# Smaller weight transfers for experts 2 to 7 and larger ones for the last two experts, in a decoder layer with routed experts

## The reference, cut to what matters

```python
h = h + merged @ w_out[l]                       # the mixer's end
logits = xt @ w_router + b_router               # 32 experts, 4 per token
top_val, top_idx = lax.top_k(logits, TOP_K)
gates = jax.nn.softmax(top_val)
def expert_block(xb, e):
    hdn = xb @ w_up[e] + b_up[e]                # 1024 -> 2048
    x_glu = jnp.minimum(hdn[:, :D_FF], 7.0)
    x_lin = jnp.clip(hdn[:, D_FF:], -7.0, 7.0)
    act = x_glu * sigmoid(1.702 * x_glu) * (x_lin + 1.0)
    return act @ w_down[e] + b_down[e]          # 1024 -> 1024
h = h + sum over the 4 experts of gate * expert(h)
out = rms_norm(h)[:, 16:]
```

## Time and profile before

| | before |
|---|---|
| median of 3 runs | 1183.54 us |
| profiled execution | 1183.1 us, span 1181.2 us |
| granted TensorE clock, mean | 0.992 |
| PE busy | 1146.4 us (97%) |
| DVE, ACT busy | 228.2 us (19%), 188.3 us (16%) |
| queue of SP (q1) | 439.19 MB, 88.1% of 16 engines' span |
| waits of PE's products for transfers (L881, L900) | 14.0 us in all, none before 700 us |

### The profile page before, as it was taken

One profiled execution on the slowest core, in us unless ns is written; L12 is line 12 of the kernel. 1 busy time (PEld: TensorE's weight loads), 2 busy tenths in 40 slices (PEclk: granted clock), 3 DMA queues, 4 the chain that ended last, 5 costly groups with the idle time before them and its releaser, 6 DMA issues.

```text
span 1181.2 us, 13320 instructions
## 1 busy us (share of the span) xinstructions
PE 1146.4 (97%) x5598; PEld 532.9 (45%) x5598; DVE 228.2 (19%) x527; ACT 188.3 (16%) x406; POOL 0.2 (0%) x4
## 2 busy tenths in 40 slices
PE   9999999999999999999999999999999999998996
PEld 7767888855343333333343433333333333333332
DVE  4555620114111111111111111111111111111112
ACT  2257620002011110101010111101010101010102
POOL 0000000000000000000000000000000000000000
PEclk9999999999999999999999999999999999999999
DMA  9834434487999999999999999999999999999996
GB/s 378 341 148 179 150 110 166 151 336 295 396 414 436 432 427 432 432 431 432 433 432 431 433 433 428 435 433 427 434 435 427 434 434 428 434 434 427 428 426 261
DMA packets 26128, 442.03 MB, mean 374 GB/s; under 512 B 4144, under 2 KB 4656, under 8 KB 7408
## 3 DMA queue, kind: packets, MB, share of 16 engines
q1 hardware_dynamic: 23472, 439.19, 88.1%
q10 hardware_dynamic: 2624, 2.39, 0.6%
HBM read 440.52 MB, written 1.05 MB: 374 GB/s over the span
## 4 chain that ended last, share of the span: by engine, by line
PE 73%; DMA 25%; ACT 1%; DVE 0%; issue 0%; ACTq 0%; SPq 0%; another core or an unknown queue 0%; DVEq 0%
PE ps L881 28%; DMA ring<-in_w_exp_dram 17%; PE ps L900 12%; PE ps L539 11%; DMA work<-in_w_exp_dram 8%; PE ps L868 4%; PE ps L856 3%; PE ps L748 2%; PE ps L811 2%; PE ps L831 2%; PE ps L772 1%; PE ps L616 1%; ACT work L1298 1%; PE ps L890 1%; PE ps L582 1%; PE ps L862 1%
## 5 line engine op out<-in xcount | busy, mean ns | idle before, releaser
L881 PE MATMUL ps<-ring,work 128*64 128x512 f32 x1536 | 347.7, 604 | 10.9 <-DMA ring<-in_w_exp_dram 10.9
L881 PEld LDWEIGHTS ps<-ring,work 128*64 128x64 f32 x1536 | 111.1, 139 | 231.4 <-issue 223.9
L1736 DVE TENSOR_SCALAR work<-ps 128x512 f32<-128x512 f32 x32 | 22.1, 691 | 741.9 <-PE ps L881 741.9
L539 PE MATMUL ps<-work,ring 128*128 128x256 f32 (+2 forms) x576 | 129.6, 384 | 0.0
L900 PE MATMUL ps<-ring,work 128*64 128x512 f32 x512 | 113.6, 595 | 5.5 <-ACT work L1298 3.8
L900 PE MATMUL ps<-work 128*64 128x512 f32 x512 | 113.8, 595 | 4.2 <-ACT work L1298 3.8
L881 PE MATMUL ps<-work 128*64 128x512 f32 x512 | 116.0, 595 | 1.0 <-DMA work<-in_w_exp_dram 1.0
L539 PEld LDWEIGHTS ps<-work,ring 128*128 128x128 f32 (+1 forms) x576 | 107.1, 188 | 19.1 <-issue 1.2
L881 PEld LDWEIGHTS ps<-work 128*64 128x64 f32 x512 | 35.2, 137 | 76.8 <-issue 73.5
L900 PEld LDWEIGHTS ps<-ring,work 128*64 128x64 f32 x512 | 35.5, 137 | 73.4 <-issue 65.4
L900 PEld LDWEIGHTS ps<-work 128*64 128x64 f32 x512 | 35.2, 137 | 72.8 <-issue 62.8
(11 more groups left out here) (232 smaller groups left out, 618.0 us busy)
## 6 DMA issues: line engine op xcount, KB each, us to landing
ring<-in_w_exp_dram SPq DMA_DIRECT2D x52, 4096.0 KB, 40.6
work<-in_w_exp_dram SPq DMA_DIRECT2D x26, 4096.0 KB, 40.6
ring<-in_w_exp_dram SPq DMA_DIRECT2D x23, 2048.0 KB, 9.9
ring<-in_w_mix_dram SPq DMA_DIRECT2D x29, 1024.0 KB, 7.3
work<-in_w_exp_dram SPq DMA_DIRECT2D x10, 2048.0 KB, 12.1
work<-in_w_exp_dram SPq DMA_DIRECT2D x4, 1024.0 KB, 43.2
ring<-in_w_exp_dram SPq DMA_DIRECT2D x2, 1024.0 KB, 5.7
ring<-in_w_mix_dram SPq DMA_DIRECT2D x2, 576.0 KB, 17.8
```

Source lines behind the costliest of these rows:

```text
L539: ins = nc.tensor.matmul(ps[part:part + width, b, 0:hi - lo], wv[:, k, o:o + width], xnT[:, k, lo:hi], start=(k == 0), stop=(k == KT - 1))
L881: ins = nc.tensor.matmul(ps[CAP * c:CAP * c + CAP, b, :], xeT[:, k, CAP * (u % 2):CAP * (u % 2) + CAP], wu[:, k % SPAN, 512 * q:512 * q + ...
L1736: V.tensor_scalar(hg, ps[:, 0, :], LIMIT, None, ALU.min).then_inc(glu_ready, 1)
```

## The change

Four edits. Experts 2 and 3 are fetched slot by slot, each slot behind the wait for the same slot two experts earlier. Experts 4 to 7 are fetched in units; they leave the loop on SP and on PE, and the loop begins at expert 8 and has five rounds. The up weights of experts 30 and 31 are fetched as pairs, as those of 28 and 29 are. And `down` counts each used slot by itself, where it counted two at every second.

```diff
-            for h in range(SPAN):
-                spe.wait_ge(weights_used, M0 + h + 1)
-                spe.dma_start(RING[0][:, SLOT * h:SLOT * h + SLOT], w_exp[2, 0, :, SLOT * h:SLOT * h + SLOT])\
-                   .then_inc(unit_loaded[0], 16)
-            for n, c in [(2, c) for c in range(1, UNITS_E)] + [(3, c) for c in range(UNITS_E)]:
-                spe.wait_ge(weights_used, M0 + PER_EXPERT * (n - 2) + SPAN * (c + 1))
-                fetch(n, c)
+            for n in (2, 3):
+                for s in range(PER_EXPERT):
+                    r = UNITS_E * (n % 2) + s // SPAN
+                    spe.wait_ge(weights_used, M0 + PER_EXPERT * (n - 2) + s + 1)
+                    spe.dma_start(RING[r][:, SLOT * (s % SPAN):SLOT * (s % SPAN) + SLOT],
+                                  w_exp[n, s // 4, :, SLOT * (s % 4):SLOT * (s % 4) + SLOT]).then_inc(unit_loaded[r], 16)
+            for n in range(4, 8):
+                for c in range(UNITS_E):
+                    spe.wait_ge(weights_used, M0 + PER_EXPERT * (n - 2) + SPAN * (c + 1))
+                    fetch(n, c)
...
-            with spe.Fori(0, (E - 8) // UNROLL) as it:
+            with spe.Fori(0, PAIRED) as it:
...
-            for u in range(2):
-                for p in range(3):
+            for u in range(UNROLL):
+                for p in range(3 if u < 2 else 2):
                     spe.wait_ge(weights_used, M0 + PER_EXPERT * (E - 6 + u) + 4 * (p + 1))
-                    fetch_pair((E - 8) // UNROLL, u, p)
-            for n, c in [(E - 2, c) for c in range(4)] + [(E - 1, c) for c in range(4)] + [(E - 2, 4), (E - 2, 5)]:
-                spe.wait_ge(weights_used, M0 + PER_EXPERT * (n - 2) + SPAN * (c + 1))
-                fetch(n, c)
+                    fetch_pair(PAIRED, u, p)
+            for c in (4, 5):
+                spe.wait_ge(weights_used, M0 + PER_EXPERT * (E - 4) + SPAN * (c + 1))
+                fetch(E - 2, c)
...
                     ins = down_step(wd[:, SLOT * (t % 2):SLOT * (t % 2) + SLOT], t, actT, 3)
-                    if t % SPAN == SPAN - 1:
-                        ins.then_inc(weights_used, SPAN)
+                    ins.then_inc(weights_used, 1)
...
-            up(0, alone(a, 3), last_start, lambda k: None)
+            up(0, paired(PAIRED, 2), last_start, lambda k: None)
...
-            up(1, alone(z, 3), lambda k: None, lambda k: None)
+            up(1, paired(PAIRED, 3), lambda k: None, lambda k: None)
```

More of the change, by code:

```diff
@@ L60 @@
 UNROLL = 4
-GROUPS = E // UNROLL
+PAIRED = (E - 12) // UNROLL
 PER_EXPERT = 12
@@ L455, in fetch_pair @@
+            for n in range(4, 8):
+                for c in range(UNITS_E):
+                    spe.wait_ge(weights_used, M0 + PER_EXPERT * (n - 2) + SPAN * (c + 1))
+                    fetch(n, c)
             def fetch_pair(it, u, p):
-                spe.dma_start(PAIR[3 * (u % 2) + p], w_exp[it * UNROLL + (u + 4), p, :, :])\
+                spe.dma_start(PAIR[3 * (u % 2) + p], w_exp[it * UNROLL + (u + 8), p, :, :])\
                    .then_inc(pair_loaded[3 * (u % 2) + p], 16)
-            with spe.Fori(0, (E - 8) // UNROLL) as it:
+            with spe.Fori(0, PAIRED) as it:
@@ L460, in _ @@
                 for u in range(UNROLL):
                     for p in range(3):
-                        spe.wait_ge(weights_used, it * (UNROLL * PER_EXPERT) + (M0 + PER_EXPERT * (u + 2) + 4 * (p + 1)))
+                        spe.wait_ge(weights_used, it * (UNROLL * PER_EXPERT) + (M0 + PER_EXPERT * (u + 6) + 4 * (p + 1)))
                         fetch_pair(it, u, p)
-            for u in range(2):
-                for p in range(3):
+            for u in range(UNROLL):
+                for p in range(3 if u < 2 else 2):
@@ L910, in down, with alone @@
                     ins = down_step(wd[:, SLOT * (t % 2):SLOT * (t % 2) + SLOT], t, actT, 3)
-                    if t % SPAN == SPAN - 1:
-                        ins.then_inc(weights_used, SPAN)
-            def alone(n, landings):
+                    ins.then_inc(weights_used, 1)
+            def alone(n):
+                landings = 1 if n < 2 else 3 + (min(n, 8) // 2 - 1)
                 def unit_of(c):
                     r = UNITS_E * (n % 2) + c
-                    pe.wait_ge(unit_loaded[r], 16 * (landings + (n >= 2 and r == 0)))
+                    pe.wait_ge(unit_loaded[r], 16 * landings)
                     return RING[r]
@@ L996, in first_between @@
                                              start=False, stop=True, skip_group_check=True)
-            up(0, alone(0, 1), first_start, first_between)
+            up(0, alone(0), first_start, first_between)
             pe.wait_ge(route_ready, 1)
@@ L1005, in _ @@
             turn_act()
[L1006 to L1012, removed]
+            down(0, alone(0))
+            odd(1, alone(1))
+            for n in range(2, 8, 2):
+                even(n, alone(n))
+                odd(n + 1, alone(n + 1))
+            with pe.Fori(0, PAIRED) as it:
                 for u in range(UNROLL):
-                    n = it * UNROLL + (u + 4)
+                    n = it * UNROLL + (u + 8)
                     if u % 2 == 0:
@@ L1018, in _ @@
                         odd(n, paired(it, u))
-            even(E - 4, paired((E - 8) // UNROLL, 0))
-            odd(E - 3, paired((E - 8) // UNROLL, 1))
+            even(E - 4, paired(PAIRED, 0))
+            odd(E - 3, paired(PAIRED, 1))
             pe.wait_ge(flag_ready, 1)
@@ L1042, in _ @@
             turn_act()
-            up(1, alone(z, 3), lambda k: None, lambda k: None)
+            up(1, paired(PAIRED, 3), lambda k: None, lambda k: None)
             pe.wait_ge(gpickT_ready, a + 1)
             pe.wait_ge(actT_ready, 2 * a + 2)
-            last_unit = alone(a, 3)
+            last_unit = alone(a)
             wd = last_unit(4)
```

## The result

The changed kernel takes 1185.25 us (median of 20 runs) against 1183.12 for the kernel before (median of 20 runs): +2.1 us, ratio 1.0019 with a 95% interval of 1.0013 to 1.0025. One of the changed kernel's 20 runs took 6719 us, in the slow state, and is left out of the ratio. The forecast was no change (1183.5). The time lies inside the range given, but the kernel has become slower by a small and clear amount, and that was not forecast.

A forecast was written before the change was run, and what follows sets the result against it. The prediction took the stream of weights to bound the kernel from about 290 us. Slots -2.2, units +1.0, instruction blocks +0.4, pairs' rate -0.4 and late wait +1.2 sum to 0.0: 1183.5 us, range 1181.0 to 1186.3.

The forecast's parts named there:

- What bounds the kernel: From about 290 us one unbroken stream of weights; PE waits for landings: 2.47 us a slot, 4.90 a unit, 9.71 a pair.
- Slots for experts 2 and 3: Early stream, 286 to 350 us: fetching slot by slot makes expert 4's first two units land earlier, -2.2 us (bounds 0, -4.4).
- The hole at 304: Early stream, between expert 0's last up step (ends 299.24) and first down step (304.8): the worst hole in the stream's work.
- Experts 4 to 7: Units instead of pairs, written out before the loop: +1.0 us for the transfers, +0.4 for further instruction blocks.
- The units' rate: Experts 4 to 7: 22 units replace 11 pairs, at 9.80 against 9.71 us per 4 MB: +1.0 us.
- their earlier issue: Units of experts 4 to 7 are issued earlier than pairs; claimed to bring nothing more, the stream being backlogged by 13.3 us.
- hits on the last engine: Instruction blocks delaying the slowest of 16 engines, 1.7 us a hit; a quarter of one hit taken, +0.4 us.
- The tail: Experts 30 and 31's up weights as pairs: stream gains 0.4 us, PE waits for whole halves, +1.2 at the end.
- the pairs' rate: Before expert 31's second up half: four pairs replace eight units in the stream, -0.4 us.
- the fourth rival: TensorE falls to half clock after idles in the last up halves: hidden in the first, +1.7 in the second, 1185.2; chance 0.08.
- The second: Rival: small transfers gain nothing early, slots starting as late after issue as units; +2.2 us, 1185.7; chance 0.10.
- The third: Rival: two of 4 to 5 new instruction packets hit the engine already last, 1.7 each; +3.0 us, 1186.5; chance 0.11.

## Why the prediction was wrong, by its steps

**What bounds the kernel** was right. The durations of 2.47, 4.90 and 9.71 us came back within 0.02 in the changed kernel, and wherever the stream moved at its end, the time moved: in all twelve profiles with expert 31's up weights in units, the span ends 15.3 to 15.4 us behind the landing of expert 31's third down slot (1164.79 to 1169.74).

**Slots for experts 2 and 3: -2.2 predicted, +0.3 measured (+0.1 alone), not told from zero.** This is the step that failed, and the size of its miss is more than the whole result. The prediction let slots 2 to 8 follow the first without a hole, and the ninth start 3.1 us after its issue. In the kernel with the slots alone, the ninth slot:

```profile
305.12 0.33 SPq L451 DMA_DIRECT2D ring<-in_w_exp_dram  x1
ring<-in_w_exp_dram SPq DMA_DIRECT2D x1, 1024.0 KB, 7.7
```

It lands at 312.8; the slot before it had landed at 308.4, so 4.4 us lie between them, and 7.7 - 2.5 = 5.2 us passed from issue to work, not 3.1. In the eight profiles with slots it landed 6.9 to 7.7 us after its issue. In the changed kernel the same slot took 6.9, 4.4 of them waiting, behind an eighth slot that had landed 1.5 us late itself. The second slot was late in all seventeen profiles that have one, by 0.4 to 1.6 us, mostly 1.0 to 1.5. The changed kernel's slots lost more beside the packet at 335 us (two landings late by 0.7 each; the last slot of expert 3 stands 1.5 behind the pace). Together: 1.25 (second slot) + 0.4 (eighth and ninth, beyond the 1.1 in the prediction) + 1.5 (beside the packet) + 0.15 (the other slots at 2.48 instead of 2.47), less 0.3 for a first slot that came earlier, is 3.0 us, and by so much expert 3 ended later than predicted.

The hole at 304 is 5.6 us without any freed slot, since PE then does bias and transposes. Smaller transfers did not close a hole in which nothing is freed, and behind it they ended no sooner than the unit: the tenth slot landed at 314.2 to 315.3 us (eight profiles), the unit in the place of the ninth and tenth at 313.7 to 314.9 (ten). Why the ninth slot came 1.4 to 2.5 us later behind the eighth than a backlogged slot, in seven of the eight, is not isolated: its queue had run down to its last transfer, and one packet of instructions began at 305.4 to 307.8 in each of these profiles. The windows say it in one number. 286 to 350 us, first with the slots alone, then with experts 4 to 7 in units alone (405 GB/s before):

```profile
286.00:350.00 64.00, 62.02 (x307) 22.41 (x304) 7.13 (x15) 7.29 (x14) 0.00 (x0) 1.00 1.00 406
```

```profile
286.00:350.00 64.00, 62.02 (x307) 22.40 (x304) 7.12 (x15) 7.29 (x14) 0.00 (x0) 1.00 1.00 411
```

At 64 us, 1 GB/s is 0.15 us. Without either part the profiles have 405 to 409 (the kernel before once more: 407), with the slots and pairs from expert 4 on 406 to 408: the slots return nothing that can be seen. Units for expert 4, whose first was issued two up steps before the pair would have been, return 0.6 to 0.9 where the slots are absent (411 in both profiles). The prediction had seen that gain and booked it under the slots.

**Experts 4 to 7: +1.0 and +0.4 predicted, +0.7 measured.** The sum was too high and the parts were not as predicted. The units' rate (+0.9 in the landings) and their earlier issue (-0.6 to -0.9) about cancel. What is left is the code: 4 packets at 0.17 us is +0.7, as the written-out code alone measured (+0.6). This is argued and not isolated, since the same part measured 0.0 on the kernel before. The prediction gave the earlier issue nothing because, of 13.3 us from issue to landing, less than half was the transfer; but a pair takes 9.71 of them. It took the packets for rare events of 1.7 us and looked for "hits on the last engine". Over a whole stream it is an average: steps move from one execution to the next, and more packets make more of them.

**The tail: +0.8 predicted (1.2 - 0.4), +1.1 measured.** The mechanism was right in each of its waits. The changed kernel's trace gives 0.9 for the chain where 1.2 stood, and 0.2 instead of 0.4 for the pairs' rate. The half clock in up 30 (the fourth rival) is seen in four of the six profiles with both experts' pairs (one of the changed kernel's own two), but it is hidden as the rival said: the last half begins there 0.2 us behind its pair instead of 0.05. In one of the average's four differences (1.4) the stores of the output have a part of 0.6.

**The rivals.** The second (slots gain nothing, 1185.7) came within 0.5 us of the time, and was given 0.10. Its mechanism for the slots is the one seen; that its sum of +2.2 meets the +2.1 so closely is partly luck, since it has +1.0 and +0.4 where +0.7 was measured and nothing for the stores (0.6 us). The third had the right cause, the instruction blocks, with the wrong arithmetic: four packets cost 0.7 us, not 3.4. What the trace of before would have shown in time: the step behind the second slot, 1.2 us, stood in it and was named in the prediction, but no price was taken for it. A misreading changed nothing: the 0.47 us before the 16 instructions at 1148.73 is a wait for one up unit, the last, and not for two.

## What to carry to other kernels

When a stream of transfers bounds a kernel, find what frees its buffers before cutting transfers smaller: a hole in which nothing is freed stays. Code fetched during the stream shares its engines, so written-out code cost time here (+3.8 us for 33 packets instead of 12) though PE was not seen to wait for instructions; a short loop bought 1.0 us, more than any change of transfer size. And a wait that covers two transfers instead of one costs most near the end, where the work behind it has no slack: 0.9 us here.

## What the runs showed of the hardware

- Each 16 KB packet of instructions fetched during a backlogged stream of weights cost 0.17 us of the kernel's time on average (5 to 33 packets, -1.0 to +3.8 us), and took 0.9 to 1.1 us of its engine. PE was never seen to wait for one. The Trainium skill ("Runtime: NRT & Kernel Launch", Instruction fetch mechanics) calls the fetch hidden; for PE these traces agree. Of the transfers beside it the section says nothing, and they were held up.
- The ninth slot of expert 2, issued 5.8 us behind the eighth, landed 6.9 to 7.7 us after its issue (eight profiles); expert 2's first slot landed 4.6 to 5.2 us after its own. Backlogged, a slot takes 2.48.
- A pair's 16 counts lay 1.8 us apart with 5 packets fetched during the stream and 6.6 with 33, and the transfer landed with the last of them.
- Slots of 1 MB ran at 2.47 to 2.49 us each with others queued behind them, 1% slower than units (4.90 for 2 MB).
- With both experts' up weights as pairs, idles of 2.0, 2.1, 2.5 and 2.7 us in up 30 were followed by 32 instructions in 8.7 to 8.8 us (granted clock 0.81 in the first two of these profiles), and idles of 1.9 and 2.1 us by the same in 7.09; the length of the idle alone does not tell which.
